# Steps of the block inverse placed between parts of the linear units, and query and key norms over 16 columns

## The reference, cut to what matters

```python
def gated_delta_rule(q, k, v, g, beta):
    q = l2_normalize(q) * (dk ** -0.5)
    k = l2_normalize(k)
    ...
    a = jnp.where(strict, jnp.einsum('nbhid,nbhjd->nbhij', k_beta, k) * decay, 0.0)
    t_inv = lax.linalg.triangular_solve(a + eye, jnp.broadcast_to(eye, a.shape), ...)
    u = t_inv @ (v * beta[..., None])
    w = t_inv @ (k_beta * jnp.exp(gc)[..., None])
    ...
    _, o = lax.scan(step, S0, (q_dec, k_dec, u, w, intra, g_last))
```

## Time and profile before

| | |
|---|---|
| median of 3 runs | 1967.79 us (1965.06 to 1971.36) |
| time of the profiled execution | 1973.12 us |
| its span | 1971.4 us |
| TensorE busy | 1835.6 us (93%) |
| VectorE busy | 1579.6 us (80%) |
| ScalarE busy | 703.5 us (36%) |
| GpSimd busy | 1046.6 us (53%) |

### The profile page before, as it was taken

How to read it: one execution, slowest core, us unless ns; L and a number is a source line. 1 busy time by engine, 2 the same in 40 slices (tenths; PEclk the granted TensorE clock), 3 DMA queues, 4 the chain that set the end, 5 groups by cost and what they waited for, 6 DMA issues and landing times.

```text
span 1971.4 us, 28772 instructions
## 1 busy us (share of the span) xinstructions
PE 1835.6 (93%) x10239; PEld 1584.9 (80%) x10239; DVE 1579.6 (80%) x2571; ACT 703.5 (36%) x1121; POOL 1046.6 (53%) x649
## 2 busy tenths in 40 slices
PE   6998869999999999999999999999999998988885
PEld 4776747999999899999978887878887676766764
DVE  5975867968989798888489999999997968757656
ACT  2342232433333344444333333333333433224441
POOL 1332225478888655565567666666764552344001
PEclk7998879999999999999999999999999999999888
DMA  8241332489999879988899999999995121200011
GB/s 346 88 166 59 131 147 75 134 300 314 312 315 305 279 262 317 312 294 306 305 361 352 356 352 354 355 353 350 364 355 202 57 96 54 75 22 3 1 56 51
DMA packets 159917, 440.47 MB, mean 223 GB/s; under 512 B 13648, under 2 KB 62928, under 8 KB 156752
## 3 DMA queue, kind: packets, MB, share of 16 engines
q1 hardware_dynamic: 64400, 254.71, 36.9%
q0 software_dynamic: 36864, 134.23, 18.2%
q10 hardware_dynamic: 58560, 50.34, 7.8%
HBM read 386.80 MB, written 52.43 MB: 223 GB/s over the span
## 4 chain that ended last, share of the span: by engine, by line
PE 70%; DVE 15%; issue 5%; POOL 4%; ACT 3%; DMA 2%; ACTq 0%; DVEq 0%; SPq 0%; PEldq 0%; POOLq 0%
PE PS L940 33%; PE PS L1147 25%; PE PS L1110 4%; POOL w_lo L832 3%; DVE arena L1784 1%; DVE arena L1975 1%; PE PS L1182 1%; ACT w_hi L1361 1%; PE PS L955 1%; DVE arena L1743 1%; PE PS L1173 1%; POOL arena L881 1%; PE PS L994 1%; DMA xres<-in_x 1%; DMA arena<-in_expert_u_rows,arena 1%
## 5 line engine op out<-in xcount | busy, mean ns | idle before, releaser
L832 POOL TENSOR_TENSOR w_lo<-raw,w_hi 128x1024 fp32r<-128x1024 f32 x300 | 723.8, 2413 | 795.0 <-ACT w_hi L1361 749.8
L1361 ACT ACTIVATE w_hi<-raw 128x1024 fp32r<-128x1024 f32 x332 | 351.9, 1060 | 989.3 <-PE PS L940 631.2
L940 PE MATMUL PS<-act_hi,w_hi 128*128 128x384 f32 (+1 forms) x1632 | 602.9, 369 | 29.7 <-DVE act_lo L1756 14.7
L940 PE MATMUL PS<-act_hi,w_lo 128*128 128x384 f32 (+1 forms) x1632 | 586.6, 359 | 0.0
L940 PE MATMUL PS<-act_lo,w_hi 128*128 128x384 f32 (+1 forms) x1632 | 586.3, 359 | 0.0
L940 PEld LDWEIGHTS PS<-act_hi,w_hi 128*128 128x128 f32 x1632 | 311.4, 191 | 78.7 <-issue 21.8
L940 PEld LDWEIGHTS PS<-act_lo,w_hi 128*128 128x128 f32 x1632 | 311.2, 191 | 25.7
L940 PEld LDWEIGHTS PS<-act_hi,w_lo 128*128 128x128 f32 x1632 | 311.9, 191 | 24.2 <-issue 1.4
L1147 PE MATMUL PS<-w_hi,act_hi 128*128 128x512 f32 x768 | 301.3, 392 | 5.5 <-ACT arena L1505 2.9
L1147 PE MATMUL PS<-w_lo,act_hi 128*128 128x512 f32 x768 | 300.1, 391 | 0.0
L1147 PE MATMUL PS<-w_hi,act_lo 128*128 128x512 f32 x768 | 300.0, 391 | 0.0
(11 more groups left out here) (330 smaller groups left out, 1901.9 us busy)
## 6 DMA issues: line engine op xcount, KB each, us to landing
raw<-in_expert_u SPq DMA_DIRECT2D x128, 512.0 KB
raw<-in_expert_v SPq DMA_DIRECT2D x128, 512.0 KB
raw<-in_w_in SPq DMA_DIRECT2D x52, 512.0 KB
arena<-in_w_ada SPq DMA_DIRECT2D x24, 1024.0 KB, 6.7
gel_d<-arena ACTq DMA_DIRECT2D x64, 384.0 KB
gates_d<-arena ACTq DMA_DIRECT2D x12, 2048.0 KB
arena<-gates_d SPq DMA_DIRECT2D x32, 768.0 KB, 7.2
arena<-gel_d SPq DMA_DIRECT2D x32, 768.0 KB
```

Of the source, the lines that this page charges most:

```text
L832: pool.tensor_tensor(w_lo[:, k % SPLIT, :], raw[:, k % RAW, :], w_hi[:, k % SPLIT, :].bitcast(F32), ALU.subtract).then_inc(lo_split, 1)
L940: mm = pe.matmul(PS[:, bank, 0:n_tok], w[:, k % SPLIT, c * P:(c + 1) * P], x[:, c, 0:n_tok], start=(i == 0 and n == 0), stop=(i == KC - 1 ...
L1361: act.activation(w_hi[:, k % SPLIT, :], raw[:, k % RAW, :], ACT.Copy).then_inc(hi_split, 1)
```

## The change

In `second_block_steps()`:

- The norms move to units 3 to 13. `square` and `sum` stand at units 3 to 10. TensorE sums the squares of one piece with four products that have one column each, so that all 8 pieces fill 2 x 16 columns. Two steps `norm_root`, after units 6 and 10, take root (ScalarE) and reciprocal (VectorE) of 16 columns. Then eight steps `spread`, after units 8, 9, 10, 11, 12, 12, 13 and 13, bring the result back to 128x512: ScalarE copies it into `tmp`, TensorE multiplies it with the identity into bank 7, and `scale` on VectorE multiplies with that bank.
- `rows` goes from VectorE to ScalarE, but for three fills. `rows` and `products` stand at units 15 to 20; pieces 1 and 2 have both at the same unit.
- Units 21 to 31 are cut into 4 parts of 6 matmuls (`part`), and all 56 `M` and `X` steps of the inverse stand between these 44 parts, 1.27 of them after each.
- The attention no longer stands in the inverse. It begins after it, with two slots between every two of the 16 steps from `tokens` to `scan`. Five slots of logits instead of 23 stand before `solve` 0.

```diff
+PARTS = 4
+INVERSE_FROM = 21
+ROWS_AT = (15, 17, 18, 19)
+DECAY_AT = (16, 17, 18, 20)
...
+    inverse = inverse_steps()
+    share = len([st for st in inverse if st[0] != "mask"]) / (PARTS * (32 - INVERSE_FROM))
+    owed = 0.0
+    for w in range(32):
+        if w >= INVERSE_FROM:
+            for k in range(PARTS):
+                steps.append(("part", w, k))
+                owed += share
+                while inverse and (owed >= 1 or inverse[0][0] == "mask"):
+                    owed -= inverse[0][0] != "mask"
+                    steps.append(inverse.pop(0))
+        if 3 <= w < 11:
+            steps.append(("square", w - 3))
         steps.append(("unit", w))
         if 1 <= w <= 12:
             steps.append(("tanh", w - 1))
         if w <= 12:
             steps.append(("conv", w))
-        if 12 <= w < 20:
-            steps.append(("sum", w - 12))
+        if 3 <= w < 11:
+            steps.append(("sum", w - 3))
+        if w in (6, 10):
+            steps.append(("norm_root", w // 10))
+        for n, at in enumerate((8, 9, 10, 11, 12, 12, 13, 13)):
+            if at == w:
+                steps += [("spread", n), ("scale", n)]
         if w == 13:
             steps.append(("rates", 0))
         if w == 14:
             steps.append(("rates_turned", 0))
-        if w == 16:
+        if w == 15:
             steps.append(("cumulate", 0))
...
+        if w in ROWS_AT:
+            steps.append(("rows", ROWS_AT.index(w)))
+        if w in DECAY_AT:
+            steps.append(("products", DECAY_AT.index(w)))
+            steps.append(("decay", DECAY_AT.index(w)))
+    steps += inverse
...
+        if (kind, n) != ("read", 0):
+            attend()
         steps.append((kind, n))
...
+        attend()
@@ TensorE
                 if kind == "sum":
-                    squares(32 + n, 1, 12 + n, ones)
+                    if n % 4 == 0:
+                        pe.wait_ge(rms_ready, 12 + n // 4)
+                    pe.wait_ge(sq_ready, 32 + n + 1)
+                    for q in range(TB):
+                        mm = pe.matmul(PS[:, 6, 4 * n + q:4 * n + q + 1], sq[:, n % 2, q * P:(q + 1) * P], ones[:, 0:1],
+                                       start=True, stop=True)
+                    mm.then_inc(sq_used, 1)
+                if kind == "spread":
+                    pe.wait_ge(spread_ready, SPREADS + n + 1)
+                    if n:
+                        pe.wait_ge(norm_ready, n)
+                    for q in range(TB):
+                        mm = pe.matmul(PS[:, 7, q * P:(q + 1) * P], tmp[:, n % 2, q * P:(q + 1) * P], ident[:, :],
+                                       start=True, stop=True)
+                    mm.then_inc(spread_ps, 1)
@@ ScalarE
-                if kind == "sum":
-                    root(12 + n, 1)
+                if kind == "norm_root":
+                    own = slice(16 * n, 16 * n + 16)
+                    act.wait_ge(sq_used, 32 + 4 * (n + 1))
+                    act.activation(nmax[:, own], PS[:, 6, own], ACT.Sqrt, bias=eps).then_inc(rms_ready, 1)
+                if kind == "spread":
+                    act.wait_ge(rinv_ready, 13 + n // 4)
+                    if n >= 2:
+                        act.wait_ge(spread_ps, SPREADS + n - 1)
+                    act.activation(tmp[:, n % 2, :].rearrange("p (a b) -> p a b", b=P),
+                                   prec[:, 4 * n:4 * n + 4].unsqueeze(2).to_broadcast([P, TB, P]), ACT.Copy
+                                   ).then_inc(spread_ready, 1)
+                if kind == "rows":
+                    act.wait_ge(rate_ready, 1)
+                    if tb:
+                        wait_full(act, "br", tb - 1)
+                    for h in range(GH):
+                        k = 4 * tb + h
+                        act.activation(h4(M1[:, 0, :])[:, h, :], upper[:, :], ACT.Copy, scale=rate[:, k:k + 1]).then_inc(rows_in, 1)
+                        act.activation(h4(M1[:, 1, :])[:, h, :], ident[:, :], ACT.Copy, scale=beta[:, k:k + 1]).then_inc(rows_in, 1)
@@ VectorE
+                if kind == "norm_root":
+                    own = slice(16 * n, 16 * n + 16)
+                    dve.wait_ge(rms_ready, 13 + n)
+                    v.reciprocal(prec[:, own], nmax[:, own]).then_inc(rinv_ready, 1)
                 if kind == "scale":
-                    if n:
-                        invert(12 + n, n, norm_ready)
-                    else:
-                        invert(12, 8, x1_ready)
+                    dve.wait_ge(spread_ps, SPREADS + n + 1)
                     v.scalar_tensor_tensor(out=cv[:, n, :], in0=cv[:, n, :], scalar=float(P) ** -0.5 if n < 4 else 1.0,
-                                           in1=rinv, op0=ALU.mult, op1=ALU.mult).then_inc(norm_ready, 1)
+                                           in1=PS[:, 7, :], op0=ALU.mult, op1=ALU.mult).then_inc(norm_ready, 1)
```

More of the change, by code:

```diff
@@ L85, in attend, with inverse_steps @@
             steps.append(("probs", i - 1))
-    for w in range(28):
-        if 12 <= w < 20:
-            steps.append(("square", w - 12))
+    def inverse_steps():
+        done = [("mask", 0, 0), ("mask", 0, 1)]
+        for level in range(LEVELS):
+            for what, tb in (("M", 0), ("M", 1), ("X", 0), ("M", 2), ("X", 1), ("M", 3), ("X", 2), ("X", 3)):
+                done.append((what, level, tb))
+                if what == "M" and 4 * level + tb + 2 < 4 * (LEVELS - 1):
+                    done.append(("mask", level + (tb + 2) // 4, (tb + 2) % 4))
+        return done
+    inverse = inverse_steps()
[11 more added lines that the diff above has]
+            steps.append(("square", w - 3))
         steps.append(("unit", w))
@@ L100, in second_block_steps @@
             steps.append(("rates_turned", 0))
-        if w == 16:
+        if w == 15:
             steps.append(("cumulate", 0))
[L103 to L136, removed]
+        if w in ROWS_AT:
[4 more added lines that the diff above has]
+    steps += inverse
+    steps += [("values", q) for q in range(TB)]
+    for kind, n in (("tokens", 0), ("tokens", 1), ("solve", 0), ("tokens", 2), ("solve", 1), ("read", 0), ("scan", 0),
+                    ("tokens", 3), ("solve", 2), ("read", 1), ("scan", 1), ("solve", 3), ("read", 2), ("scan", 2),
+                    ("read", 3), ("scan", 3)):
+        if (kind, n) != ("read", 0):
+            attend()
         steps.append((kind, n))
@@ L1221, in _ @@
                         pe.wait_ge(mx_ready, n - 33)
-                    linear(U_IN2 + n, n, unit_bank(n), split={0: 24, 32: 32}.get(n), order=X_ORDER if n == 0 else range(KC),
-                           between=both_sums if n == 0 else None)
+                    if not INVERSE_FROM <= n < 32:
+                        linear(U_IN2 + n, n, unit_bank(n), split={0: 24, 32: 32}.get(n),
+                               order=X_ORDER if n == 0 else range(KC), between=both_sums if n == 0 else None)
+                if kind == "part":
+                    if tb == 0:
+                        pe.wait_ge(p_dve, n - 1)
+                        pe.wait_ge(*lowered(U_IN2 + n))
+                    for c in range(KC // PARTS * tb, KC // PARTS * (tb + 1)):
+                        for i, (w, x) in enumerate(((w_hi, act_hi), (w_lo, act_hi), (w_hi, act_lo))):
+                            mm = pe.matmul(PS[:, unit_bank(n), :], w[:, n % SPLIT, c * P:(c + 1) * P], x[:, c, :],
+                                           start=(c == 0 and i == 0), stop=(c == KC - 1 and i == 2))
+                    if tb == PARTS - 1:
+                        mm.then_inc(unit_done, 1)
                 if kind == "rates":
@@ L2452, in _ @@
             dve.wait_ge(gn_done, GH)
-            invert(20)
+            dve.wait_ge(rms_ready, 15)
+            v.reciprocal(rinv, rms[:, 0, :]).then_inc(rinv_ready, 1)
+            dve.wait_ge(rinv_ready, 15)
             for c in range(8):
```

20 lines of the change are left out of this document (6 added, 14 removed).

## The result

The changed kernel takes **2031.4 us** (median of 5 runs, 2027.7 to 2040.7) against 1967.8: a ratio of 1.0323, 95% interval 1.0297 to 1.0349. It is slower, as forecast, but by 63.6 us where 35 were forecast, and it lies above the range (1966 to 2022 us). Its profiled execution took 2040.7 us, span 2038.9.

What follows compares the result with a forecast made beforehand. TensorE was taken to bind up to the inverse, with both TensorE and VectorE near full behind it. Section A at +34 and B+C at +1 (208 against 206.9) gave +35 on 1967.8: 2003 us, range 1966 to 2022.

Steps and rivals of the forecast that it cites:

- C: Attention and last steps after the inverse: 74 us of VectorE work at a busy share of 0.78, 95 us, bounds 74 to 110.
- A: Units 4 to 20 with norms, rates, rows and products: +34 us, bounds +24 to +42.
- B: Units 21 to 31 in parts with the inverse between them: 113 us, bounds 100 to 118.
- Section A, the waits: Behind units 8 to 13 TensorE waits for ScalarE's late copy at each spread: +25.9 us, 8 of them the spreads' own work.
- the term of +10: In the norms TensorE's granted clock falls behind four gaps of 4.5 us and more, 2.5 us each; bounds 0 and 18.
- The sums, +5.4: Added one-column sums of squares on TensorE at units 3 to 7: four at 1.2 us and 0.6 for the first.
- -11.2: In the norms, eight old sums of 1.4 us each removed from TensorE.
- (rates): Running sums behind unit 15 alone: TensorE waits about 5.4 us where it waited 4.63, +1 us.
- (rows): ScalarE's rows ahead of products of pieces 1 and 2: 3.2 us wait each, 6.4 instead of 3.2, +3 us.
- Payback: Attention as tight as VectorE's work (74 us), parts cost nothing between them (100 us): -9 in total, 1959 us; chance 0.12.
- TensorE does not stop: At the norms spreads cause no wait, cost 8 instead of 25.9 us, and the clock holds: +7, 1975 us; chance 0.10.
- The third rival: Clock stays down in the norms (+42) and the attention section is loose (110 us): +58, 2026 us; chance 0.15.

Runs made afterwards that it cites:

- Experiment 2: Changed kernel with ScalarE's copy for each spread a unit earlier and the spreads one behind each of units 8 to 15: 2005.5 us, ratio 1.0184.
- experiment 5: On top of experiment 2, ScalarE's rows of pieces 1 and 2 stand behind the products of the piece before: 1996.4 us, ratio 1.0119.
- Experiment 3: Changed kernel with matmuls whose result nobody reads ahead of TensorE's waits for the spreads' copies: 2025.9 us, ratio 1.0287.
- experiment 4: Changed kernel with no attention slot between the last steps; all 36 slots follow behind them: 2049.7 us, ratio 1.0402.
- experiment 9: On top of experiment 2, VectorE's 32 maxima over rows of logits replaced by writes of zero: 1998.5 us, ratio 1.0136.
- experiment 10: Experiment 4 with three matmuls of unused result ahead of each attention turn: 2048.8 us, ratio 1.0395; attention alone 79.8 us against 85.4.
- experiment 1: Changed kernel with norms, rates, rows and products kept, but from unit 28 on the step list of the kernel before: 2008.6 us, ratio 1.0188.
- experiment 6: On top of experiment 2, ScalarE's token copies, squares and root one attention slot later, VectorE's low part at its slot's end: 2002.9 us, ratio 1.0151.
- experiments 8 and 12: Score products asked for a slot early: on top of experiment 2, 2030.3 us; on the kernel with hidden norms and old order from unit 28, 1987.3 us.

## Why the prediction was right in its sign and wrong in its size

The profiled executions differ by 67.5 us where 35 were forecast. Of the 32.5 us between, C makes 22.4, A 7.7 and B 2.6 (what lies outside the three takes 0.3 off).

**Section A, the waits: right.** TensorE stands still for each spread, for the reasons given. From unit to unit the six gaps are 3.9, 4.1, 5.9, 5.7, 6.3 and 5.8 us, 31.7 in all; 4.8 of them is the spreads' own work at a low clock (14.1 us instead of 8 x 1.17), so 26.9 stand against the forecast 25.9. Behind units 8 to 10 TensorE has a sum of 0.8 us to do in the gap, so the gaps are not idle throughout: the waits for a copy are 1.4 to 3.7 us. The waits ahead of the products are 7.1 us (6.4 forecast), the one for the rates 6.0 (5.4). Experiment 2 takes 27 to 30 us out with nothing but the places of copies and spreads, and experiment 5 another 9 to 13.

**Section A, the clock: the term of +10 was mis-sized.** It counted four falls of 2.5 us, only behind waits of 4.5 us and more. The clock falls in every one of the six gaps, those of 3.9 and 4.1 us at units 8 and 9 included, and behind the waits ahead of the products. Units 9 to 13 and the rates take 40.95 us against 6 x 5.47, 8.1 more; the spreads 4.8, units 4 and 16 3.6, the products of pieces 1 and 2 3.9: 20.4 us. The kernel before had 3.0 of such time itself, in the sum at 1649.37 us (1.95 instead of 0.87) and in the unit behind it (7.42 instead of 5.47). The term is therefore +17.4, just under its upper bound of 18. Experiment 3 shows 12.5 us of it directly. The sums, +5.4 in the forecast, are four of 0.79 us in this section, 3.2: by luck that hid a part of the miss. With these the section closes: -11.2 + 3.2 + 26.9 + 17.4 + 1.4 (rates) + 3.9 (rows) = 41.6 us, against the measured 41.7.

**The table load.** ScalarE's `tanh` behind unit 11 starts at 1629.18, 0.02 us after its table load of 1.28 us from 1627.88. The Trainium skill, ScalarE: Activation LUTs, section What ACT_TABLE_LOAD costs, adds a drain of about 1380 ns to each; this trace shows none, as the one before.

**Section B: right.** 115.6 us against 113: a part 1.60 us with its switch, `M` 0.61, a wait of 3.7 us for the first mask. In the chain the parts take 71.0 us (73 with the switches in the forecast), the inverse 40.0 (35): small misses, partly against each other.

```profile
1738.29 1.40 PE PS L1239 x6
1739.68 3.70 issue
...
1850.96 1.59 PE PS L1239 x6
1852.56 0.62 PE PS L1190 x8
```

**Section C: the step that failed.** "With two slots to a step I take 0.78: 95 us", bounds 74 and 110. VectorE's work was right (72.2 us against 74). The share was not: 0.62, and 117.4 us lies above the upper bound, which had been taken from shares of the kernel before as if VectorE's work set the length and only the tightness were open. It does not set it. Alone, the attention takes 85.4 us for 49.9 us of VectorE's work (experiment 4), and 12.3 us less of that work shorten the mixture by 5 to 10 (experiment 9). What sets it is the serial chain through TensorE, VectorE and ScalarE, with TensorE in it partly at the low clock (0.80 in C, 0.60 in the attention alone), which its waits bring about (experiment 10). The sum also used the share on other work than it was read from: the 18 us of subtractions were taken out of VectorE's work, but the 54.6 of 70.0 us that make 0.78 contain them. Without them it is 36.4 of 70.0, 0.52, and TensorE, busy for 58.4, was the fuller engine in that stretch. The 0.78 of the kernel before came from the steps of the inverse between the slots. They gave the engines something to do in the attention's waits: without the 60 us of 11 units, the kernel before needs 146.9 us for inverse, attention and last steps together; the changed one needs 55.6 for the inverse among its parts and 117.4 for the rest, 173. "What the parts win by keeping TensorE fed, the attention loses by standing alone": it loses 26 us more than they win, and experiment 1 gives 27 by the times of the kernels.

**The rivals.** Payback and "TensorE does not stop" are refuted by the chain. The third rival (clock down, C loose) was the right one: A +42 as measured; its C of 110 was 7 us short. It had 0.15 and should have had the most.

**Open.** Which of the chain's waits could be taken out of the mixture is not settled: loosening three places brought nothing that can be told from noise (1.4 us in the section, experiment 6) and asking for the scores earlier cost 26 us in the section. How the 117.4 us divide between chain and clock in the mixture was not measured either; experiment 10 bounds it only for the attention alone.

## What to carry to other kernels

A share of busy time read from one mixture can't be moved to another. Where, as here, an engine is at 0.6 and no other is near full, look for a chain that sets the length; what hides it is the independent work between its links: ask how long each chain takes alone, and how much independent work is left beside it after the edit. And where an engine at its limit takes an operand from another engine, ask for the operand one step of the list before its use: the same work with the copies a unit early and the spreads one to a unit was 27 us faster; with the rows early too and the old order behind it, it was 0.5% faster than the kernel before. It is the producer's step that moves: score products asked for before VectorE had worked off those of the pair before held up TensorE's queue and cost 24 and 28 us (experiments 8 and 12).

## What was not expected of the hardware

TensorE's granted clock fell behind a wait of 1.44 us. Behind unit 8 the engine made one-column products for 0.8 us and stood still for 1.44 us, both at a granted clock of 1.00. Then the spread's products took 1.67 us, at 0.64, instead of 1.17, and the unit behind them 6.58 instead of 5.47: 1.6 us more than the wait itself. The fall doesn't always come at once: behind the wait of 2.23 us after unit 12 the first spread's products still ran at 1.00 (1.17 us), and the second's, 0.87 us of wait later, at 0.50 (2.04 us). Matmuls with no use in the same waits held the clock at 1.00 (experiment 3), in the attention alone at 0.97 instead of 0.60 (experiment 10).
